# Joining products and turning T by transposes in the recurrent stage of a two-layer encoder on one core

## The reference, cut to what matters

```python
def rwkv7_step(state, inp):
    r, w, k, v, kk, a = inp
    sa = jnp.einsum('...vk,...k->...v', state, -kk)
    state = (state * w[..., None, :]
             + sa[..., :, None] * (kk * a)[..., None, :]
             + v[..., :, None] * k[..., None, :])
    y = jnp.einsum('...vk,...k->...v', state, r)
    return state, y
```

## Time and profile before

| What | Value |
|---|---|
| Median of three runs | 1822.62 us (1816.73 to 1828.1) |
| The profiled execution, its own time | 1826.01 us |
| Its span in the profile | 1824.2 us |
| TensorE busy | 1745.9 us, 96% of the span, 14193 matmul records |
| VectorE, ScalarE, GpSimd busy | 960.5, 765.9 and 171.3 us |
| Mean granted TensorE clock | 0.991 |
| The four pairs, from the first Gram product to the first step of the last chain | 167.17 to 382.78 us, 215.61 us |

### The profile page before, as it was taken

The page is one execution under the profiler, slowest core; times in us unless marked ns, Lnnn a source line. Parts: engine busy times, 40 slices in busy tenths (PEclk is TensorE's granted clock), DMA queues, the critical chain, the costliest instruction groups (busy, mean ns, idle before and its releaser), DMA issues.

```text
span 1824.2 us, 32058 instructions
## 1 busy us (share of the span) xinstructions
PE 1745.9 (96%) x14193; PEld 1438.6 (79%) x14193; DVE 960.5 (53%) x1257; ACT 765.9 (42%) x1180; POOL 171.3 (9%) x175
## 2 busy tenths in 40 slices
PE   6998888889999999999999999999999999999999
PEld 5877777777887788888887887668888788888887
DVE  5477666436434455624545245884534356633652
ACT  4343444434544344413433234884554343422340
POOL 1001221221010000000000022450010000000000
PEclk9999999999999999999999999999999999999999
DMA  7210000124331223323322222003421222222221
GB/s 244 82 46 2 4 4 4 43 77 162 139 111 39 82 81 98 110 94 107 100 70 93 93 92 93 1 1 116 139 73 67 92 93 92 93 93 92 93 98 65
DMA packets 96454, 149.42 MB, mean 82 GB/s; under 512 B 3479, under 2 KB 50170, under 8 KB 96314
## 3 DMA queue, kind: packets, MB, share of 16 engines
q1 hardware_dynamic: 94727, 142.29, 23.7%
q0 software_dynamic: 1296, 4.95, 0.8%
q10 hardware_dynamic: 291, 0.12, 0.0%
HBM read 145.25 MB, written 2.10 MB: 81 GB/s over the span
## 4 chain that ended last, share of the span: by engine, by line
PE 86%; DVE 6%; ACT 3%; issue 2%; DMA 1%; POOL 1%; POOLq 0%; SPq 0%; DVEq 0%; ACTq 0%
PE PS L371 69%; PE PS L1026 2%; PE PS L1040 2%; PE PS L550 1%; PE PS L1575 1%; DVE SS L1868 1%; DVE WLO L337 1%; PE PS L1067 1%; PE PS L656 1%; ACT WHI L331 1%; PE PS L1059 1%; PE PS L1544 1%; DVE AT L1880 1%; PE PS L1699 1%; PE PS L919 1%
## 5 line engine op out<-in xcount | busy, mean ns | idle before, releaser
L337 DVE TENSOR_TENSOR WLO<-WRAW,WHI 128x2048 fp32r<-128x2048 f32 (+1 forms) x131 | 294.6, 2251 | 450.6 <-ACT WHI L331 450.6
L331 ACT ACTIVATE WHI<-WRAW 128x2048 fp32r<-128x2048 f32 (+1 forms) x132 | 248.2, 1881 | 400.9 <-PE PS L371 383.6
L371 PE MATMUL PS<-HIS,WHI 128*128 128x512 f32 x856 | 333.8, 390 | 1.5 <-DVE SM L2027 1.5
L371 PE MATMUL PS<-HIS,WLO 128*128 128x512 f32 x856 | 333.0, 389 | 0.0
L371 PE MATMUL PS<-LOS,WHI 128*128 128x512 f32 x856 | 333.0, 389 | 0.0
L371 PE MATMUL PS<-WHI,HIS 128*128 128x512 f32 x608 | 241.1, 396 | 0.0
L371 PE MATMUL PS<-WHI,LOS 128*128 128x512 f32 x608 | 237.6, 391 | 0.0
L371 PE MATMUL PS<-WLO,HIS 128*128 128x512 f32 x608 | 237.6, 391 | 0.0
L371 PEld LDWEIGHTS PS<-HIS,WHI 128*128 128x128 f32 x856 | 160.7, 188 | 35.1 <-DVE SM L2027 1.7
L371 PEld LDWEIGHTS PS<-LOS,WHI 128*128 128x128 f32 x856 | 160.7, 188 | 33.5 <-issue 0.2
L371 PEld LDWEIGHTS PS<-HIS,WLO 128*128 128x128 f32 x856 | 160.7, 188 | 33.4
(11 more groups left out here) (293 smaller groups left out, 2494.5 us busy)
## 6 DMA issues: line engine op xcount, KB each, us to landing
WRAW<-ffn_w_up SPq DMA_DIRECT2D x88, 512.0 KB, 4.5
WRAW<-ffn_w_down SPq DMA_DIRECT2D x20, 1024.0 KB, 5.1
WRAW<-cross_wkv SPq DMA_DIRECT2D x16, 1024.0 KB, 5.1
WRAW<-diff_w_in SPq DMA_DIRECT2D x12, 1024.0 KB, 5.0
WRAW<-ab_w_in SPq DMA_DIRECT2D x10, 1024.0 KB, 5.4
WRAW<-cross_wq SPq DMA_DIRECT2D x8, 1024.0 KB, 5.1
WRAW<-cross_wo SPq DMA_DIRECT2D x8, 1024.0 KB, 5.1
X<-x SPq DMA_DIRECT2D x8, 512.0 KB, 5.0
```

Of the source, the lines that this page charges most:

```text
L331: A.e.activation(part(WHI[place(i)], i), part(WRAW[i % 2], i), ACT.Copy).then_inc(S("w_hi"), 1)
L337: V.e.tensor_tensor(part(WLO[place(i)], i), part(WRAW[i % 2], i), part(WHI[place(i)], i).bitcast(F32), ALU.subtract).then_inc(S("w_lo"), 1)
L371: mm = e.matmul(o, l, r, start=(si == 0 and kk == 0 and q == 0), stop=(si == len(steps) - 1 and kk == nk - 1 and q == 2))
```

## The change

The diff, by parts:

1. T is no longer computed as a product. In levels 1 to 4 the new `turn_u_pe` transposes UU by four full 128x128 transposes per direction into bank 4, and the new `turn_u_act` copies them to TT. Both directions use that one bank, so the second turn waits for the first copy (`p_t0`). In a level TensorE now does both X products, the turn of direction 0, the side work 2 lv, the turn of direction 1, the chain step, both U products, side work 2 lv + 1 and the chain step.
2. In levels 1 to 4 the X products are laid over all four quarters of the array (`level_units`), the results go to two banks, and the copies and masks read these two banks (`level_banks`, `by_bank`). The U products of all levels now stand alone, on two quarters.
3. R and P are one product of 64x128 (`rp`), since B's triangle and the turned beta stand side by side in GB (instead of GBR and BPD). GKA moves to BPD's place.
4. The two directions' K triangles are added once by GpSimd (`gram_sum_pool`, 128x512), and K.V is 16 products instead of 32.
5. A chain step is one group with one semaphore: VectorE waits for y and then adds state and y.

```diff
@@ chain_pe
         else:
-            e.wait_ge(S("c_state"), j * (STEPS - 1) + i - 1)
+            e.wait_ge(S("c_yfree"), j * STEPS + i - 1)
...
-                    mm = e.matmul(PS[half(hh), 4, d * HD:d * HD + HD], PT[half(hh), d, o[d][0], :],
+                    mm = e.matmul(PS[half(hh), 5, P + d * HD:P + d * HD + HD], PT[half(hh), d, o[d][0], :],
...
-            mm.then_inc(S("c_mm"), 1)
-        if i > 1:
-            e.wait_ge(S("c_yfree"), j * STEPS + i - 1)
@@ pair_pe
+    def turn_u_pe(e, d):
+        for q in range(NT):
+            mm = e.transpose(PS[:, 4, q * P:q * P + P], UU[:, d, 2 * q:2 * q + 2, :].rearrange("p c k -> p (c k)"), ident)
+        mm.then_inc(S(f"p_tn{d}"), 1)
...
+                    for x, q, c, u in level_units(lv):
+                        mm = e.matmul(PS[xs(c), 2 * d + (x ^ c), q * CH:q * CH + CH], AI[xs(x), d, u, :],
+                                      UU[xs(x), d, 2 * q + c, :], start=True, stop=True)
                 mm.then_inc(S("p_x"), 1)
+            if lv > 0:
+                turn_u_pe(e, 0)
             side_pe(T, j, 2 * lv)
+            if lv > 0:
+                e.wait_ge(S("p_t0"), j * (LV - 1) + lv)
+                turn_u_pe(e, 1)
...
-                        if lv < LV - 1:
-                            mm_t = e.matmul(PS[xs(1 - y if lv == 0 else y), 2 * d + 1, u * CH:u * CH + CH], XX[xs(y), d, u, :],
-                                            TT[xs(y), d, u, :], start=True, stop=True)
...
+                    for x, q, c, u in level_units(lv):
+                        mm = e.matmul(PS[xs(c), 2 * d + (x ^ c), q * CH:q * CH + CH], TT[xs(c), d, 2 * q + x, :],
+                                      XX[xs(c), d, 2 * q + (x ^ c), :], start=True, stop=True)
@@ tail
-        tail(6, 0, 0, v, gkr, "bank", "")
-        tail(6, 0, 1, v, gkr, "", "")
+        e.wait_ge(S("p_gks"), j + 1)
+        tail(6, 0, 0, v, gks, "bank", "")
...
-            mm = tail(4, d * 256, d, w, gbr, "each", "each")
-        mm.then_inc(S("p_r"), 1)
+            for t in range(NT):
+                for x in range(2):
+                    for hh in range(2):
+                        mm = e.matmul(PS[half(hh), 4 * (1 - d) + x, t * P:t * P + P], w(d, hh, t, x),
+                                      GB[xs(x), d, hh * NT + t, :], start=True, stop=True)
+            mm.then_inc(S("p_rp"), 1)
...
-        tail(0, 0, 0, w, bp, "each", "each")
-        tail(0, 256, 1, w, bp, "each", "each").then_inc(S("p_p"), 1)
@@ pair_act
         for lv in range(LV):
+            if lv > 0:
+                turn_u_act(e, j, lv, 0)
             side_act(A, j, 2 * lv)
+            if lv > 0:
+                turn_u_act(e, j, lv, 1)
@@ pair_pool
+        e.wait_ge(S("p_gfree"), 2 * j + 2)
+        e.tensor_tensor(GKR[:, 0, :, :], GKR[:, 0, :, :], GKR[:, 1, :, :], ALU.add).then_inc(S("p_gks"), 1)
```

More of the change, by code:

```diff
@@ L148, in build @@
     r3 = r2 + 38912
-    names5 = ["GBR", "GKA", "GKR", "AI", "UU"]
-    U5 = {n: sb(n, [P, 2, 8, CH], r3 + 4096 * i) for i, n in enumerate(names5)}
-    GBR, GKA, GKR, AI, UU = (U5[n] for n in names5)
+    GB = sb("GB", [P, 2, 8, P], r3)
+    names5 = ["", "", "GKR", "AI", "UU"]
+    GKR, AI, UU = (sb(n, [P, 2, 8, CH], r3 + 4096 * i) for i, n in enumerate(names5) if n)
     TT = sb("TT", [P, 2, 8, CH], r3 + 20480)
@@ L868, in xs, with level_units, by_bank, level_banks @@
         return slice(CH * x, CH * x + CH)
+    def level_units(lv):
+        return [(x, q, c, 2 * q + (c ^ (x & (lv - 1) & 1))) for q in range(NT) for c in range(2) for x in range(2)]
+    def by_bank(tile):
+        return tile.rearrange("p (q b) k -> p b q k", b=2)
+    def level_banks(d):
+        return PS[:, 2 * d:2 * d + 2, 0:256].rearrange("p b (q k) -> p b q k", k=CH)
     def chunk(t, x):
@@ L1023, in pair_pe @@
                     e.wait_ge(S("p_qfree"), j)
[L1024 to L1027, removed]
+                if lv == 0:
+                    for u in range(8):
+                        for x in range(2):
+                            mm = e.matmul(PS[xs(x), 2 * d, u * CH:u * CH + CH], AI[xs(x), d, u, :], U0[xs(x), d, u, :],
+                                          start=True, stop=True)
+                else:
+                    for x, q, c, u in level_units(lv):
+                        mm = e.matmul(PS[xs(c), 2 * d + (x ^ c), q * CH:q * CH + CH], AI[xs(x), d, u, :],
+                                      UU[xs(x), d, 2 * q + c, :], start=True, stop=True)
                 mm.then_inc(S("p_x"), 1)
+            if lv > 0:
+                turn_u_pe(e, 0)
             side_pe(T, j, 2 * lv)
+            if lv > 0:
+                e.wait_ge(S("p_t0"), j * (LV - 1) + lv)
+                turn_u_pe(e, 1)
             if j > 0 and 1 <= 2 * lv <= STEPS:
@@ L1037, in pair_pe @@
                     e.wait_ge(S(f"p_t{d}"), j * (LV - 1) + lv)
[L1038 to L1041, removed]
-                        if lv < LV - 1:
-                            mm_t = e.matmul(PS[xs(1 - y if lv == 0 else y), 2 * d + 1, u * CH:u * CH + CH], XX[xs(y), d, u, :],
-                                            TT[xs(y), d, u, :], start=True, stop=True)
-                mm_u.then_inc(S(f"p_un{d}"), 1)
-                if lv < LV - 1:
-                    mm_t.then_inc(S(f"p_tn{d}"), 1)
+                if lv == 0:
+                    for u in range(8):
+                        for x in range(2):
+                            mm = e.matmul(PS[xs(x), 2 * d, u * CH:u * CH + CH], TT[xs(x), d, u, :], XX[xs(x), d, u, :],
+                                          start=True, stop=True)
+                else:
+                    for x, q, c, u in level_units(lv):
+                        mm = e.matmul(PS[xs(x), 2 * d + (x ^ c), q * CH:q * CH + CH], TT[xs(c), d, 2 * q + x, :],
+                                      XX[xs(c), d, 2 * q + (x ^ c), :], start=True, stop=True)
+                mm.then_inc(S(f"p_un{d}"), 1)
             side_pe(T, j, 2 * lv + 1)
+            if lv == 0:
+                e.wait_ge(S("p_gfree"), 2 * j + 1)
             if j > 0 and 2 * lv + 1 <= STEPS:
-                if lv == 0:
-                    e.wait_ge(S("p_gfree"), 2 * j + 1)
                 chain_pe(e, j - 1, 2 * lv + 1)
@@ L1198, in side_act @@
             for d in range(2):
-                i = e.activation((BPD, KPD)[s - 6][:, d, :, :], PS[:, 6 + d, :].rearrange("p (t k) -> p t k", k=P), ACT.Copy)
+                if s == 6:
+                    i = e.activation(units(GB[:, d, :, CH:P]), PS[:, 6 + d, :].rearrange("p (t b k) -> p b t k", b=2, k=HD),
+                                     ACT.Copy)
+                else:
+                    i = e.activation(KPD[:, d, :, :], PS[:, 6 + d, :].rearrange("p (t k) -> p t k", k=P), ACT.Copy)
             i.then_inc(S("p_tokfree"), 1)
@@ L1323, in pair_pool @@
             bonus_value_pool(G.e, j - 1)
+            gram_sum_pool(G.e, j)
     def part2(b, s):
```

57 lines of the change are left out of this document (31 added, 26 removed).

## The result

The changed kernel takes 1801.15 us (median of four runs, 1799.05 to 1807.05) beside 1821.34 us for the kernel before on the same chip (four runs, 1816.73 to 1828.1). The ratio is 0.9885 with an interval of 0.9857 to 0.9914: some 20 us, 1.15% faster. That is clear of no change, but 1% lies inside the interval, so whether it is more than the 1% that I gave as the limit of such a measurement is not shown; "within 1%" had the chance of 0.71. The forecast was 1810, so the kernel is 9 us faster than I said, within the range and nearer to rival B's 1799.5.

The account below looks back on a forecast made before the run. TensorE was taken as bound by array work and almost as hard by instruction supply; 14 us of gaps gained, 2 lost, 12 net, 12.5 with the clock, gave 1810 us against 1822.6, range 1797 to 1824.

Parts of the forecast that it names:

- within 1%: Whole kernel: the measured time differs from the kernel before by no more than 1%, 18 us; chance 0.71.
- rival B: Recurrent stage: issue gaps all but vanish (6 us left) and both low-clock windows go; 1799.5 us, chance 0.22.
- Issue rows: Recurrent stage: TensorE's waits for instructions fall from 28.5 to 14.5 us, 14 us gained.
- Waits for TT: Level 4: TensorE waits for ScalarE's copies of the turns, 0.7 us per pair, 1.7 in the first.
- First pair without chain steps: First pair, levels 2 and 3: no chain step covers ScalarE's copy, a wait of about 0.5 us each.
- U in levels 1 to 4: Levels: U alone on two quarters doesn't gain, 64 records at 29 ns, 1.85 us.
- All other array work: Per pair: level 0 0.2 us less, level 4 0.15 more, K.V 0.5 less; sum -0.6 us.
- no block takes less than about 3.7 us, whatever is in it: Recurrent stage: TensorE's instruction supply is a second bound, in blocks of some 255 instructions.
- Rival C: Recurrent stage: gaps have nothing to do with instruction count and stay, only +2 us remain; 1824.5 us, chance 0.19.
- the array gains nothing: Levels 1 to 3: X, transposes and U after the change take 3.89 us against 3.85 before.
- It fits in three pairs, with nothing to spare: Levels 1 to 3: ScalarE's copies, 2.9 us, finish within TensorE's 3.0 us of other work.
- The clock: Recurrent stage: two half-clock windows cost 1.7 us each; fewer gaps may save a third of that.

Follow-up runs that it names:

- u_two_quarters: Changed kernel with U's results in levels 1 to 4 put into the half of their operands, so U uses two quarters (values wrong): 1809.2 us, ratio 0.9904.
- turn_between: Changed kernel with the first turn of U moved between the two X products: 1801.51 us, ratio 0.9871.
- the repeat: The changed kernel run again word for word, as yardstick: 1802.05 us, ratio 0.9877.
- fill_sparse: Changed kernel with one unused 128x512 product more per pair at the end of level 1, where instructions are few: 1806.82 us, ratio 0.9903.
- late_slab: Changed kernel with the load of the first ab_w_out slab held until the last pair's bonus sum: 1798.85 us, ratio 0.9852.

## Why the prediction was right and wrong

The sum, term by term, in the stage (before against after in the profiled executions; minus is faster):

| Term | Forecast, us | Measured, us |
|---|---|---|
| Issue rows | -14 | -17.6 |
| Waits for TT | +3.8 | +5.1 (+2.2 of it in level 4), and 2.3 of broken series |
| First pair without chain steps | +1 | within the row above |
| U in levels 1 to 4 | 0 | 16 x -0.86 = -13.8 |
| All other array work | -2.4 | about -0.7 (what is left) |
| Stage | -12 | -24.5 |

**The bound.** Right: most of the gaps are the supply of instructions, "no block takes less than about 3.7 us, whatever is in it". The shortest distance between the ends of two such gaps is 3.45 us (354.28 to 357.73 us), not counting the last one, which is in part the wait for Q's copy, so 3.7 is a little high. The 44 packets were forecast at 44; the gaps left stand in the tails and in the Gram products behind them; filler work is free there and not elsewhere. Here the Trainium skill's page "Runtime: NRT & Kernel Launch", section "Instruction fetch mechanics", calls the cost of a block's boundary mostly hidden: the gap inside Q of 1.36 us that vanished behind 1.06 us of filler shows that it isn't where a block has 2 to 3 us of work. Rival C is out with that and with the fall from 28.5 to 10.9 us.

**The size of the issue term.** 10.9 us are left, not 14.5. Between the pairs they are 1.52 + 0.47, 1.36 + 0.99 and 0.79 + 2.70, and at the end of the last 0.59 + 1.26 + 1.24: 2.0, 2.4, 3.5 and 3.1 us. Forecast were 2.9 in each tail, 11.5 in all, and 3 more for the longest piece and the wait behind Q. The tails' own figure was near the mean of 2.7; the 3 us on top were too many, since those pieces turned out to lie inside the four sums. Forecast windows of 50, 49, 51 and 52 us were 45.3, 47.4, 45.3 and 53.2: only the last, with the longest gap and the half clock, is as long as I said.

**The step that failed:** "U alone on two quarters (its operands and its result lie in the same half, so it doesn't gain: 64 at 29 ns, 1.85)", and from it "the array gains nothing". U takes 0.99 us. It wasn't a wrong rate; 15 to 16 ns on four quarters and 29 to 32 on two hold for the long series of 64x64 products in both kernels, at full clock. It was a line of the kernel misread, and u_two_quarters shows what the misreading was worth: 9.2 us of the stage, because 3 to 4 of the 13.8 come back as waits for TT.

**The waits for TT.** Forecast only in level 4 (0.7 per pair, 1.7 in the first) and, in the first pair, levels 2 and 3 (0.5 each). The sum of 5.1 us is near the forecast of 4.8 (with the first pair's 1.0), but its parts are not. The first pair waits 1.70 us in level 4, as forecast, and 0.81 and 0.66 in levels 2 and 3 where 0.5 each was forecast. In the later pairs level 4 has only 0.15 us each instead of 0.7: the products with GKA (L1018) take some 2 us, so the copy of turn 0 lands before turn 1 is due (in the second pair it ends at 249.26 us and turn 1 starts at 249.46), and the 0.5 us ahead of turn 1 never comes. With U half as long TensorE arrives earlier instead in levels 2 and 3 of the second and third pair (0.36 and 0.20 us) and in level 3 of the last (0.20). That the sum fits is luck. "It fits in three pairs, with nothing to spare" would have been right for the U that I believed in: with it the list has 1.9 us in all, 1.4 of them one wait ahead of the first pair's second turn, the table load's.

**The order** (both X ahead of turn 0) brings no measurable time by itself: turn_between is the same within 1 us, though its profile has some 3 us more work in the stage. The gain comes from T by transposes, the four quarters and the joined products.

**The clock.** I allowed 0.5 us for fewer windows of half clock, and counted two in the stage; the first 3.4 us of the stage were a third, unchanged, and the one at 382.9 us lies just behind its end. In this profile two of the three later ones went: the last chain's first nine records took 2.27 us where they had taken 3.43, and no window came at 366 us where before one stood at 389.7. Two windows of 3.4 us at half speed cost up to 3.4 us, most of the 4.4 us behind the stage. It is the luck of one execution in part, since the repeat has such a window again (at 368.0 us, nine records in 3.50 us). My reading that the window comes with the longest gap doesn't hold either: gaps of 2.98 and 3.13 us had none behind them.

**The range** held, and in part by luck: it reached down to 1797 for rival B, whose gaps of 6 us didn't come about (10.9 stay), and what filled the room was mostly U, which no rival had. B's own sum is wrong as well: 22.5 + 4 - 2 is 24.5, which gives 1798.1 and not 1799.5.

**A slip in the sum.** For R and P the text has 1.9 us against 2.05 and calls it "no more than 0.1 less"; by its rates (128 at 15 ns, 64 at 32) it would be 0.1 more. The measured 29 ns for L1112 makes it 1.86, about the same as before.

Not settled: about 2 us in "all other array work", what brings a window of half clock, and whether the weight load's traffic or its instructions lengthen the longest gap. A kernel in which X and U of all four quarters share one bank wasn't tried.

## What to carry to other kernels

In a stretch of small products look at "issue" rows and at their spacing in instructions before you ask which engine is late: here a block of 255 instructions took no less than 3.5 to 4 us, so fewer instructions shorten a dense stretch, and big products with few instructions can be put into it for nothing. Lay a series of 64x64 products so that all four pairings of operand half and result half occur in it: that halved the time of X and of U. Crossing the halves alone isn't enough (X of before crossed them and stood on two quarters), and a second bank alone isn't either; every series on four quarters here also writes two banks, so whether one bank would do is not shown. And read each output's partition from the kernel's own line, letter by letter, before a rate is put to it; count too what a shorter step uncovers, since a third of U's gain was lost again, most of it to waits.

## What the runs showed of the hardware that was not expected

- Checks of a satisfied semaphore between small products cost TensorE about 0.1 us for each instruction that the profile counts (512 of them cost 49 us, in one run). Whether a single check costs as much was not tried.
- Full fp32 transposes of 128x128 in a row start 110 to 165 ns apart (four in 0.44 to 0.66 us) in the middle of a level; in the earlier trace rows it is 128.
- 32 records that start after a wait take 0.69 us and 64 in a row 0.99.
- The gap at the last pair's start went from 2.70 us to 1.60 when a load of 1 MB was held back.
- Windows of half clock come and go between kernels that differ by a few instructions: a clock of 1.00 behind gaps of 2.98 and 3.13 us in turn_between and fill_sparse, 0.51 behind one of 2.70 in the changed kernel, and in late_slab none there but one of 0.50 at 363.8 to 367.2 us. Each costs up to 1.7 us, as much as some of the edits compared here.
